# A hybrid attention, SSD and expert trunk on one core: the unused products of TensorE set to zero

## The reference

```python
h = rmsnorm(x, g_mix[l])
proj = h @ w_in[l]                       # 1024 x 6408
o_a = diff_attention(q, k, v, ...)       # 4 heads, block-causal
o_b = pool_mixer(proj[..., COL_POOL:COL_Z], w_pool_group[l], pool_scale[l])
o_c = ssd_mixer(...)                     # chunked scan
merged = sum of sigmoid gates times (o_a, o_b, o_c) @ w_branch[l]
x = x + merged @ w_mix_out[l]
x = x + mem_cross_attention(rmsnorm(x, g_xattn[l]), mem_n, w_xq[l], w_xkv[l], w_xo[l])
x = x + hierarchical_moe(rmsnorm(x, g_moe[l]), ...)   # 16 experts, two per row
return rmsnorm(x, g_final)
```

## Time and profile before

| what | us |
|---|---|
| median of 3 runs (523.77 to 526.60) | 525.15 |
| the profiled execution's own time | 526.87 |
| its span, first to last instruction | 525.1 |
| PE busy | 503.5 |
| DVE busy | 246.5 |
| ACT busy | 197.4 |
| POOL busy | 15.6 |

### The profile page before, as it was taken

One profiled execution on the slowest core, in us unless ns is written; L12 is line 12 of the kernel. 1 busy time (PEld: TensorE's weight loads), 2 busy tenths in 40 slices (PEclk: granted clock), 3 DMA queues, 4 the chain that ended last, 5 costly groups with the idle time before them and its releaser, 6 DMA issues.

```text
span 525.1 us, 7201 instructions
## 1 busy us (share of the span) xinstructions
PE 503.5 (96%) x2814; PEld 338.5 (64%) x2814; DVE 246.5 (47%) x466; ACT 197.4 (38%) x349; POOL 15.6 (3%) x30
## 2 busy tenths in 40 slices
PE   8999999899999999999989899999999999999982
PEld 7998998678888888898978534433443344333331
DVE  3764599866788689965563711102011111111113
ACT  6455757545626455454555212111211111111113
POOL 2000100000130000000010000000000000000000
PEclk9999999989999999999999899999999999999997
DMA  7887647433555458975996599999999999999982
GB/s 249 277 278 225 196 143 246 134 107 103 169 163 182 161 158 252 359 278 163 347 406 219 227 332 392 401 403 404 402 399 401 400 403 404 402 399 400 399 303 84
DMA packets 65978, 149.28 MB, mean 284 GB/s; under 512 B 8790, under 2 KB 12052, under 8 KB 65940
## 3 DMA queue, kind: packets, MB, share of 16 engines
q1 hardware_dynamic: 65924, 148.76, 78.8%
q10 hardware_dynamic: 16, 0.00, 0.0%
HBM read 147.69 MB, written 1.05 MB: 283 GB/s over the span
## 4 chain that ended last, share of the span: by engine, by line
issue 46%; PE 39%; DVE 10%; ACT 2%; DMA 1%; SPq 0%; POOLq 0%; POOL 0%; ACTq 0%; DVEq 0%
PE bank L1377 11%; PE bank L1378 11%; PE bank L1379 11%; DVE wl L903 4%; PE bank L1400 1%; DMA raw<-in_w_in 1%; DVE xc L919 1%; PE bank L1489 1%; ACT wh L559 1%; PE bank L1512 1%; PE bank L1486 1%; DVE big L949 1%; DVE al L889 1%; DVE big L1199 1%; DVE small L1188 0%
## 5 line engine op out<-in xcount | busy, mean ns | idle before, releaser
L903 DVE TENSOR_TENSOR wl<-raw,wh 128x1024 fp32r<-128x1024 f32 (+1 forms) x80 | 94.5, 1197 | 38.7 <-ACT wh L559 37.2
L559 ACT ACTIVATE wh<-raw 128x1024 fp32r<-128x1024 f32 (+1 forms) x80 | 82.2, 1042 | 71.3 <-PE bank L1379 52.0
L1377 PE MATMUL bank<-wh,ah 128*128 128x512 f32 (+2 forms) x248 | 94.8, 382 | 0.0
L1379 PE MATMUL bank<-wh,al 128*128 128x512 f32 (+2 forms) x248 | 93.2, 376 | 0.0
L1378 PE MATMUL bank<-wl,ah 128*128 128x512 f32 (+2 forms) x248 | 93.2, 376 | 0.0
L1304 DVE TENSOR_TENSOR kT<-bank,normg 64x512 f32<-64x512 f32 x16 | 11.0, 689 | 124.1 <-ACT normg L797 124.1
L1379 PEld LDWEIGHTS bank<-wh,al 128*128 128x128 f32 x248 | 46.6, 188 | 8.6
L1377 PEld LDWEIGHTS bank<-wh,ah 128*128 128x128 f32 x248 | 46.7, 188 | 8.1
L1378 PEld LDWEIGHTS bank<-wl,ah 128*128 128x128 f32 x248 | 46.7, 188 | 7.9
L1377 PE MATMUL bank<-ah,wh 128*128 128x256 f32 x160 | 45.9, 287 | 1.7 <-DVE wl L903 1.0
L1378 PE MATMUL bank<-al,wh 128*128 128x256 f32 x160 | 45.2, 283 | 0.0
(11 more groups left out here) (333 smaller groups left out, 835.5 us busy)
## 6 DMA issues: line engine op xcount, KB each, us to landing
raw<-in_w_in SPq DMA_DIRECT2D x48, 512.0 KB, 4.7
gates<-in_w_exp_gate SPq DMA_DIRECT2D x15, 512.0 KB, 11.7
gates<-in_w_exp_up SPq DMA_DIRECT2D x15, 512.0 KB, 13.4
wh_raw<-in_w_exp_gate SPq DMA_DIRECT2D x15, 512.0 KB, 11.6
wl_raw<-in_w_exp_up SPq DMA_DIRECT2D x15, 512.0 KB, 11.3
raw<-in_w_branch SPq DMA_DIRECT2D x12, 512.0 KB, 4.5
conv_raw<-in_w_exp_up SPq DMA_DIRECT2D x10, 512.0 KB, 11.1
raw<-in_w_exp_gate SPq DMA_DIRECT2D x10, 512.0 KB, 10.7
```

The costliest lines, as they stand in the source:

```text
L559: act.activation(dst, src, ACT.Copy, scale=scale).then_inc(done, 1)
L903: dve.tensor_tensor(wl[:, n % RING, 0:sz], raw[:, n % RING, 0:sz], wh[:, n % RING, 0:sz].bitcast(F32), ALU.subtract)\
L1377: pe.matmul(dst, st[0], mv[0], start=start, stop=False, skip_group_check=True)
L1379: return pe.matmul(dst, st[1], mv[0], start=False, stop=stop, skip_group_check=True)
```

## The change

Every count in the table becomes zero, so that `keep_warm` issues nothing anywhere. No wait, no real product, no transfer and no order between real steps is altered.

```diff
-WARM = (10, 6, 5, 6, 14, 0, 4, 1, 9, 6)
+WARM = (0, 0, 0, 0, 0, 0, 0, 0, 0, 0)
```

## The result

The changed kernel takes 528.03 us in the median of 14 runs (526.04 to 530.70), the kernel before 525.65 us in 14 runs beside them (523.77 to 529.68). The ratio is 1.0038, 95% interval 1.0020 to 1.0056, that is +2.0 us (1.05 to 2.9) on 526. The change makes the kernel a little slower, less than the 0.5% that the prediction set as a mark. The two profiled executions are closer than the medians: 527.31 against 526.87 us, spans 525.6 and 525.1. Of the fourteen runs after, the profiled one is the third shortest.

What follows compares the result with a forecast made beforehand. PE was taken as the pace up to 300 us, then PE and DMA side by side. Start +1.5, cross attention +1.8 and products -0.1 give +3.2 us on 525.15, forecast 528.3 us, range 524.6 to 532.5.

Steps and rivals of the forecast that it cites:

- The products themselves hold up nothing: At all places of the removed products: their 92 records delay almost no real work, gains sum to 0.1 us.
- rival C: Chain of waits is right: products between xq chunks and ahead of xo0 delay work, 2.43 us return, 522.7 us; chance 0.05.
- Start: Chunks 0 and 1: without products the clock is still low from 11.83 us, +1.5 us, bounds 0 and 2.8.
- chunk 1 starting after 16 us: Sign in the changed trace that the forecast is right at the start; chunk 1 at 15.4 us would show it wrong.
- Cross attention: After the scores: PE idles 4.24 us, the clock falls, L1652 ends late, +1.8 us, bounds 0 and 2.9, or 4.6.
- the sum: Whole kernel: 1.5 + 1.8 - 0.1 = +3.2 us, put on the median of 525.15 us.
- the dip at 294 us: Ahead of the ranks: idle time becomes 2.3 instead of 1.93 us; the profiled execution already dips, so nothing added.
- Passing to the end: Whole kernel: every microsecond that PE's real work loses before 300 us arrives at the end.
- Rival D: Start and after the scores: transposes don't raise the clock, +4.9 to +7.6 us, near 531.4 us; chance 0.13.
- Rival B: Clock hardly cares: start or cross-attention term goes, the other halves, +0 to +1.7 us, 525.1 to 526.9; chance 0.22.
- The idle time of 1.0 us: Ahead of 261.8 us, between the xq chunks: said to be under half the shortest idle before a dip; nothing added.

Runs made afterwards that it cites:

- e4: Kernel before without its three small groups (between the xq chunks, ahead of xo0, ahead of the ranks): 526.15 against 526.09 us, ratio 1.0013.
- e3: Kernel before without the 21 products of the start: 527.95 against 526.09 us, ratio 1.0039.
- e2: Kernel before with only the 14 products after the scores kept, the other 32 removed: 529.26 against 526.09 us, ratio 1.0051.
- e1: Kernel before without the 14 products after the scores: 527.69 against 526.09 us, ratio 1.0027.
- e5: Kernel before with 7 instead of 14 products after the scores: 526.48 against 526.10 us, ratio 1.0013.
- e7: Kernel before with 8 products instead of 1 ahead of the ranks: 526.23 against 526.10 us, ratio 1.0009.
- e8: Kernel before with 8 products instead of 1 ahead of the ranks and 9 more at 103 us: 525.62 against 526.10 us, ratio 0.9999.
- e9: Kernel before with 9 more products at 103 us, where PE waits for L1069: 525.46 against 526.19 us, ratio 0.9989.
- e10: Kernel before with 6 more products between the two halves of the router logits: 526.86 against 526.19 us, ratio 1.0011.
- e6: Kernel before with 20 more products ahead of xo0: 532.36 against 526.10 us, ratio 1.0118.

## Why the prediction was right, point by point

**The whole.** Forecast 528.3 us, measured 528.03, inside the range, and slower as forecast. In the difference it was less exact: +3.2 forecast, +2.0 us (1.05 to 2.9) by the ratio. The forecast gave 0.58 to slower by over 0.5%, and the measured 0.38% lies under that mark, where it had put 0.37. That the total came within 0.3 us is in part luck: the median that it started from, 525.15 us of three runs, is 0.5 us under the 525.65 of fourteen, and that offsets a part of a sum that was 1.2 us too high.

**The products themselves hold up nothing (0.1 us).** Right. The two groups on the chain of waits are replaced by waits (e4), and rival C, the gain of 2.43 us, is refuted by e4's time; L1637 to `xo0` is 11.89 us with and without the group there.

**Start, +1.5 us.** Right in mechanism and size where it happens: +1.57 (e3) and +1.42 us (e2) at chunk 1, carried unchanged to the scores. By time e3 measures +2.1 us (0.8 to 3.2). What the prediction did not say is that it is not there in every run. In the profile after, with the same sixteen transposes in front, the clock was up before chunk 0, and the term was 0. The sign to look for, "chunk 1 starting after 16 us", failed there for that reason. I had first read this as a refutation, and put it so in the expectation of e3; three profiles decide better than one. How many of the fourteen runs after have the delay is open, because the granted clock reads 1.00 at the start in either case.

**Cross attention, +1.8 us.** Right: +2.01 in the profile after, +1.6 in e1 and in e5. The lower stretch was taken as 5.3 us from the first transpose; in the profile after it ends 277.5 - 271.7 = 5.8 us behind it. The fall itself came as I had taken it for sure, in both profiles without any products there, and none of the fourteen runs after has a mean clock above 0.982.

**Added up, too much.** The step that was wrong is the sum: I let both terms pass through to the end unchanged, and wrote of the stage behind `xo0` that nothing was to be added. I had tied the dip at 294 us to the 1.93 us of idle time ahead of the ranks; in e7, e8 and e9 PE has no such idle time and the clock falls all the same. And the table shows that this stage is not fixed. From `xo0` to the experts it takes 20.76 to 20.77 us in the three profiles in which the clock fell at the cross attention (after, e1, e5), and 21.47 to 23.53 in the eleven others (e7, e8 and e10 have more products in it). So at least 0.7 us, and 1.15 us against the profile before, of the 2.0 lost at the cross attention come back there. In those three the next low stretch covers the first four residual products (3.33 us in the rows after), where DVE's choice of experts hides it, and the second four and the gather run at full clock. In the profile before it is the other way about; in e3 both fours are slow (3.76 and 3.53 us), and the stage takes 23.20. The likely reason is that `xo0` then starts at nearly the same distance from the rise of the clock. The window 276 to 278 us has a granted clock of 0.63 in the profile after, 0.98 in e1 and 0.71 in e5, and 274 to 276 us 0.50 in all three, so the clock rose at 277.5, 276.1 and 277.2 us, and `xo0` starts 1.8, 2.3 and 1.8 us behind it. The row of the profile after:

```profile
276.00:278.00 2.00, 2.00 (x27) 2.00 (x25) 0.17 (x1) 0.43 (x2) 0.00 (x0) 0.63 0.07 27
```

The later low stretch then meets the same work each time. No run was made that forces it, and it stays argued. Nor do the timings prove the give-back by themselves. e1 and e2 split the change in two, and add up to 1.4 + 2.7 = 4.1 us against 2.0 for the whole. The difference of 2.1 us is about as large as its own uncertainty, some 2 us by an estimate from the three intervals.

**Passing to the end.** Right: e6's delay arrives whole, and the expert stage takes 216.6 to 218.8 us in every profile, without a clear trend by how late it starts. Its own spread of 2.2 us, which the prediction did not mention, is larger than either term.

**Rival D, transposes don't raise the clock.** Wrong here. In the profile after, seventeen transposes (L1389 and L1409) are all that PE did before 11.6 us, and chunk 0 ran at the upper level. They can thus be enough, though in e3 and e2 they were not. After the scores, too, the clock rose at 277.5 us, and not 5.3 us after the first product L1652 (275.34 us) as D had it. The Trainium skill, page "TensorE: Matmul & The Clock Gate", Part 4, says that the full clock does not engage for transpose mode, which does not count as busy in the same way. The profile after disagrees: behind transposes alone the records of chunk 0 are 0.12 us apart.

**Rival B** named what happened in one execution (the start's term gone, +0.5 us in the span), not in the median.

**Slips in the working.** None changed the forecast. The idle time of 1.0 us is not under half of 1.93 us (0.97); e4 measured 1.10 us there, and its clock did not fall. From 1.72 to 6.9 us it is 5.2 us, not 5.3. Half as long again as the mean of 3.4 and 5.3 us is 6.5 us, not 6.9, and the bound 2.6 us, not 2.8. The sixteen transposes could not end at 10.4 us: they took 3.68 us from 7.25 on, to 10.93. Rival B's 525.1 to 526.9 us lie wholly inside the range, which was said to leave out their far half.

## What to carry to other kernels

Work on TensorE that computes nothing can be worth its place if it stands in a wait that another engine ends: it delays nothing as long as it ends before that wait does (in e7 eight products did not), though a chain of waits may list it, and removing it turns it into a wait of nearly the same length. Price it by the real work behind the gap that would run at the lower clock, and then follow the clock onward, since a stretch lost here may move the next low stretch and give a part back. A term that comes and goes from run to run needs several profiles: one execution showed 0 us for a term that others showed at 1.4 to 1.6.

## What the runs showed of the hardware

The clock can fall without PE being idle. In the kernel after, and in e1, e5, e7 and e8, a low stretch covers the residual products that follow the router logits without a wait. The logits are 32 records of only 20 columns that stand back to back (286.95 to 290.69 in the rows after). In e9 two thirds of the 15 us from 285 on are low, with PE busy throughout:

```profile
285.00:300.00 15.00, 15.00 (x56) 9.40 (x55) 8.64 (x35) 4.60 (x8) 0.00 (x0) 0.66 0.58 222
```

With twelve records of 128 columns between the logits it stayed up in e10, in the one profile and by the clock of its runs. Why it falls at this place is not shown, as no run varied the logits alone. The busy share of the page gives no hint: PE is at 15.00 of 15 us in the row above while the clock is at 0.66.

The same code meets the clock differently in each execution: of the profiles with all products at the start, four (before, e1, e5, e6) have the 1.57 us dip at 106 us and three (e4, e7, e10) have not, behind the same 2.34 to 2.37 us of idle time. And the printed granted clock before the first change is 1.00 even where the records are 0.21 to 0.23 us apart: at the start of a trace only the spacing tells the level.
